# Normed columns kept in memory for two gate stages and the stick projections, with transposed stick queries and keys

## The reference

```python
hx = rms_norm(x, norm_g[i]) * (1.0 + scale_x) + shift_x      # layer 0: window attention, layer 1: latent attention
# both layers: o = attention(projections of hx);  y = (o * silu(hx @ W_gate)) @ W_out
x = x + gate_x * y

# second block, even mixer
hn = rmsnorm(h, norm_gain[0])
qa, ka, va, ga, qb, kb, vb, gb = split(hn @ w_in, 8)         # eight parts of 512 columns
o_a = retention(rotary(qa), rotary(ka), va)
o_b = stick_breaking(qb, kb, vb)                             # four heads of 128
mixed = concat([o_a * silu(ga), o_b * silu(gb)]) @ w_out
```

## Time and profile before

| | us |
|---|---|
| median of 3 runs | 4573.9 (4572.03 to 4575.41) |
| the profiled execution | 4582.14, of which its span is 4580.4 |
| window gate stage, first to last instruction | 635.4 to 973.8 |
| latent gate stage | 1887.9 to 2160.9 |
| stick projections | 2474.9 to 2732.9 |

### The profile page before, as it was taken

The page is one execution under the profiler, slowest core; times in us unless marked ns, Lnnn a source line. Parts: engine busy times, 40 slices in busy tenths (PEclk is TensorE's granted clock), DMA queues, the critical chain, the costliest instruction groups (busy, mean ns, idle before and its releaser), DMA issues. The chain is left out here.

```text
span 4580.4 us, 70575 instructions
## 1 busy us (share of the span) xinstructions
PE 4184.7 (91%) x29426; PEld 2468.8 (54%) x29426; DVE 1581.9 (35%) x2947; ACT 1361.1 (30%) x2322; POOL 318.1 (7%) x143
## 2 busy tenths in 40 slices
PE   7999989989989999898998988998999978888798
PEld 1447854445556666543554446443444467788443
DVE  0336642123135444322332017012222256666111
ACT  0117752212245555321222228111222121211132
POOL 0000000000000000000000000000000027565000
PEclk9999999999999999999999999998999989999899
DMA  7100020041241111001102001104111121211300
GB/s 268 61 1 4 2 84 0 0 85 47 86 125 32 32 32 32 5 0 35 57 0 74 0 1 48 45 0 175 46 46 55 51 102 41 67 50 40 138 14 23
DMA packets 158778, 229.26 MB, mean 50 GB/s; under 512 B 79750, under 2 KB 90182, under 8 KB 158536
## 3 DMA queue, kind: packets, MB, share of 16 engines
q1 hardware_dynamic: 158542, 225.78, 14.9%
HBM read 175.21 MB, written 50.54 MB: 49 GB/s over the span
## 5 line engine op out<-in xcount | busy, mean ns | idle before, releaser
L221 PE MATMUL psum<-rp_w,rp_mixed 128*128 128x512 f32 x1024 | 448.2, 596 | 6.6 <-issue 3.6
L221 PEld LDWEIGHTS psum<-rp_w,rp_mixed 128*128 128x128 f32 x1024 | 194.3, 191 | 248.3 <-issue 242.0
L1353 PE MATMUL psum<-la_kT,la_qT 96*128 96x512 f32 (+1 forms) x768 | 300.6, 528 | 15.4 <-DMA la_v<-latent_v 12.5
L2296 POOL TENSOR_TENSOR rs_kk<-rs_k,rs_k_k 128x1024 f32<-128x1024 f32 x7 | 16.5, 2362 | 3833.4 <-DVE rs_k L2640 3707.7
L1295 DVE TENSOR_SCALAR_CACHE_REDUCE la_s<-psum 128x1280 f32<-128x1280 f32 x128 | 190.9, 1492 | 238.1 <-PE psum L1353 238.1
L221 PE MATMUL psum<-output_wo,pg_oT 128*128 128x512 f32 x512 | 230.8, 610 | 12.2 <-DMA output_wo<-in_even_w_out_dram 6.0
L221 PE MATMUL psum<-output_wg,pg_xT 128*128 128x512 f32 x512 | 227.4, 602 | 7.3 <-ACT pg_xT L1927 7.3
L221 PE MATMUL psum<-retention_w,sp_hT 128*128 128x512 f32 x512 | 223.3, 597 | 10.2 <-ACT even_o L1656 8.7
L221 PE MATMUL psum<-retention_w,ret_hT 128*128 128x512 f32 x512 | 222.9, 596 | 3.3 <-DMA retention_w<-in_even_w_in_dram 1.7
L1283 ACT ACTIVATE la_pT<-psum 128x512 f32<-128x512 f32 x256 | 138.9, 595 | 289.0 <-PE psum L1371 289.0
L1353 PEld LDWEIGHTS psum<-la_kT,la_qT 96*128 96x128 f32 x768 | 137.1, 192 | 141.9 <-issue 129.0
(11 more groups left out here) (410 smaller groups left out, 7106.3 us busy)
## 6 DMA issues: line engine op xcount, KB each, us to landing
ada_slots<-in_ada_w_dram SPq DMA_DIRECT2D x12, 2048.0 KB, 19.5
rwkv_raw<-x_rows SPq DMA_DIRECT2D x48, 512.0 KB, 2.6
retention_w<-in_even_w_in_dram SPq DMA_DIRECT2D x8, 2048.0 KB, 13.2
rp_w<-in_odd_w_in_dram SPq DMA_DIRECT2D x4, 4096.0 KB, 29.0
output_wg<-in_ple_gate_dram SPq DMA_DIRECT2D x2, 4096.0 KB, 23.5
latent_v<-lp_v SPq DMA_DIRECT2D x10, 512.0 KB, 2.6
la_kT<-latent_kT SPq DMA_DIRECT2D x16, 320.0 KB, 4.6
la_v<-latent_v SPq DMA_DIRECT2D x16, 320.0 KB, 5.3
```

Of the source, the lines that this page charges most:

```text
L221: last = pe.matmul(out[:, c:c + w], left[:, k, :], right[:, k, c:c + w], start=(k == 0), stop=(k == kd - 1))
L1353: last = pe.matmul(s_banks[:, c:c + n], qT[:, s, q * P:(q + 1) * P], kT[:, s, c:c + n], start=True, stop=True)
L2296: eng.tensor_tensor(kk[:, :], k[s][:, :], k_k[:, :], ALU.mult).then_inc(q["kk_made"], 1)
```

## The change

It stores columns and uses them again, and drops the norm from three stages.

- `window_qkv`: the two-slot hT becomes a buffer of the layer. SP stores the columns of tiles 0 to 7 to memory; tiles 8 and 9 stay in the two slots. DVE waits for the store before it writes a slot again.
- `window_attend`: SP loads the gate's first weight half, wg0, behind its own two loads.
- `gate_and_project`: no norm. The tiles go 8, 9, 0 to 7 in the window layer. SP loads the columns of tile i into slot i % 2 once gate product i - 2 is done. The gate has two PSUM pairs, ogT two slots. PE's order becomes transposes of og(i), gate product i+2, output product i; the last tile's transposes come ahead of the output product before it, into the gate pair that is free.
- `latent_projections`: SP stores the columns of the eight x tiles, DVE waits for the store as above. `latent_attention` prefetches the first two tiles' columns behind the gate weights.
- `retention`: SP stores the columns of tiles 0 to 6; tile 7 stays in SBUF. DVE waits for the store of tile i before it makes the columns of i+1.
- `stick_projections`: no norm and no transposes. hT holds four tiles (128 x 8 x 512). v and gate are made per tile as before; q and k are made transposed, with the weight of one head stationary and 512 rows of columns streaming, straight into qT and kT.

```diff
+class Columns:
+    def load(self, sp, i):
+        sp.dma_start(self.at[:, i % 2, :, :], self.sources[i]).then_inc(self.arrived[i % 2], 16)
+    def wait(self, pe, i):
+        loads = sum(self.sources[k] is not None for k in range(i % 2, i + 1, 2))
+        if loads:
+            pe.wait_ge(self.arrived[i % 2], loads * 16)
...
 # window_qkv, SP, behind its weight loads (latent_projections: the same store ahead of each step's others)
+                for i in range(NT - 2):
+                    sp.wait_ge(hT_steps, (i + 1) * 2)
+                    sp.dma_start(hT_dram[i], hT[:, i % 2, :, :]).then_inc(hT_stored[i % 2], 16)
 # window_qkv and latent_projections, DVE, columns(i)
                     if i >= 2:
                         dve.wait_ge(kv_made, i - 1)
+                        dve.wait_ge(hT_stored[i % 2], (i // 2) * 16)
...
 # gate_and_project
-        front = Front(nc, mem, name, core, None, 0, core.banks(0, 2))
-        g_banks, ogT_banks, y_banks = core.banks(2, 2), core.banks(4, 2), core.banks(6, 2)
+        g_sets, y_banks = [core.banks(0, 2), core.banks(2, 2)], core.banks(6, 2)
+        ogT_banks = lambda i: core.banks(4, 2) if i + 1 < count else g_sets[count % 2]
...
+                weights.load(sp, late)
+                for i in range(2, count):
+                    sp.wait_ge(g_made, i - 1)
+                    columns.load(sp, i)
...
 # ACT
+                silus(0)
+                for i in range(count):
+                    if i + 1 < count:
+                        silus(i + 1)
                     move(i)
 # DVE
                 gates(0)
                 dve.wait_ge(gate_in, 16 * len(conds))
+                for i in range(count):
+                    if i + 1 < count:
+                        gates(i + 1)
                     residual(i)
 # PE
                 def output_product(i):
                     pe.wait_ge(ogT_read, i + 1)
-                    pe.wait_ge(y_steps, i * Y_STEPS)
+                    if i:
+                        pe.wait_ge(y_steps, (i - 1) * Y_STEPS + 1)
...
                 gate_product(0)
+                gate_product(1)
                 pe.wait_ge(weights.arrived["wo"], 16)
+                for i in range(count):
+                    if i < count - 1:
+                        transpose_og(i)
+                    if i + 2 < count:
+                        gate_product(i + 2)
+                    if i == count - 2:
+                        transpose_og(count - 1)
                     output_product(i)
...
 # retention, DVE, ahead of dve_columns(i + 1)
+                    dve.wait_ge(hT_stored, i * 16 + 16)
...
 # stick_projections, PE
+                def rows(n):
...
+                    product(pe, v_banks[n % 2], left, w_v[:, :, :], zv_made)
+                    product(pe, g_banks[n % 2], left, w_g[:, :, :], zg_made)
+                def turned(n):
+                    c, h, which = turns[n]
+                    if n >= 4:
+                        pe.wait_ge(turned_moved, n - 3)
+                    w = (w_q, w_k)[which]
+                    for k in range(KD):
+                        last = pe.matmul(turned_banks[n % 4], w[:, k, h * R_DIM:(h + 1) * R_DIM], hT[:, k, :], start=(k == 0), stop=(k == KD - 1))
+                    last.then_inc(turned_made, 1)
...
+                rows(0)
...
+                for n in range(len(turns) // 2):
+                    turned(n)
+                for n in range(1, X_TILES):
+                    rows(n)
+                for t in range(CHUNK):
+                    pe.wait_ge(hT_in[t], 32)
+                for n in range(len(turns) // 2, len(turns)):
+                    turned(n)
```

More of the change, by code:

```diff
@@ L373, in window_qkv @@
              "rope_k", "q_turned", "k_turned", "qT_moved", "kT_moved"))
+        hT_stored = [nc.alloc_semaphore(f"{name}_hT_stored{k}") for k in range(2)]
         cond = lambda i: 1 if i < CTX_TILES else 0
@@ L726, in _, with gate_and_project @@
                         values(u - 2)
-def gate_and_project(nc, core, name, o, tiles, layer, weights, load, gate_rows):
+def gate_and_project(nc, core, name, o, tiles, weights, late, columns, gate_rows):
     with ExitStack() as mem:
@@ L1408, in _, with retention @@
                 passes(pe, run)
-def retention(nc, core, a, weights, next_weights, o):
+def retention(nc, core, a, weights, next_weights, o, hT, hT_dram):
     name = "ret"
@@ L1451, in _ @@
                 weights.load(sp, ("w1", "w2", "w3"))
+                for i in range(X_TILES - 1):
+                    sp.wait_ge(front.hT_made, i + 1)
+                    sp.dma_start(hT_dram[i], hT[:, :, :]).then_inc(hT_stored, 16)
+                sp.wait_ge(hT_stored, (X_TILES - 1) * 16)
                 sp.wait_ge(qk_made, X_TILES)
@@ L1643, in _, with load @@
             def _(sp):
-                sp.dma_start(norm_columns[:, :], columns_of(a["norm_gain_2"][0]), allow_slow_non_contiguous=True).then_inc(norm_in, 16)
+                def load(t):
+                    sp.dma_start(hT[:, :, columns(t)], hT_dram[t]).then_inc(hT_in[t % CHUNK], 16)
+                for t in range(CHUNK):
+                    load(t)
+                sp.wait_ge(turned_made, len(turns) // 2)
+                for t in range(CHUNK, LAST):
+                    sp.wait_ge(zg_made, order.index(t - CHUNK) + 1)
+                    load(t)
@@ L1658, in _ @@
-                with act.Fori(0, X_TILES - 1) as i:
-                    front.act_stat(act, i + 1, x(i + 1))
-                    move(i)
-                move(X_TILES - 1)
+                for n, t in enumerate(order):
+                    act.wait_ge(zv_made, n + 1)
+                    act.activation(v[:, t, :], v_banks[n % 2], ACT.Copy).then_inc(v_moved, 1)
+                    act.wait_ge(zg_made, n + 1)
+                    act.activation(o[:, t, W:], g_banks[n % 2], ACT.Silu).then_inc(g_moved, 1)
@@ L1678, in _ @@
-                move(X_TILES - 1)
+                for n, (c, h, which) in enumerate(turns):
+                    if n == len(turns) // 2:
+                        dve.wait_ge(zg_made, order.index(CHUNK - 1) + 1)
+                        dve.tensor_copy(hT[:, :, columns(LAST)], last_hT[:, :, :]).then_inc(hT_in[LAST % CHUNK], 16)
+                    dve.wait_ge(turned_made, n + 1)
+                    dst = (qT, kT)[which]
+                    dve.tensor_copy(dst[:, h, c * CHUNK * P:(c + 1) * CHUNK * P], turned_banks[n % 4]).then_inc(turned_moved, 1)
@@ L2878, in program @@
             o = layer.enter_context(nc.sbuf_tensor("window_o", [P, ALL_TILES, D], F32))
+            hT = layer.enter_context(nc.sbuf_tensor("window_hT", [P, 2, KD, P], F32))
+            window_hT = nc.dram_tensor("window_hT_rows", [ALL_TILES - 2, P, KD, P], F32, kind="Internal").ap()
+            gate_tiles = [ALL_TILES - 2, ALL_TILES - 1] + list(range(ALL_TILES - 2))
+            columns = Columns(nc, "window_columns", hT, [None, None] + [window_hT[t] for t in range(ALL_TILES - 2)])
+            first = Weights(nc, layer, "window_first", {"wg0": halves("wg", a["a_w_in"][0][:, D + 2 * A_KV * A_DIM:])["wg0"]})
             with ExitStack() as keys:
```

198 lines of the change are left out of this document (83 added, 115 removed).

## The result

| | before | after |
|---|---|---|
| median, us | 4574.2 (4 runs, 4572.03 to 4575.41) | 4449.24 (4 runs, 4444.99 to 4460.8) |
| profiled execution, us | 4582.14 | 4446.34 |
| span, us | 4580.4 | 4444.3 |
| mean granted clock | 0.960 | 0.969 |

The ratio is 0.9736, with a 95% interval of 0.9721 to 0.9752: faster, by 125 us against 115 forecast.

The account below looks back on a forecast made before the run. PE, busy 91% of the span, was taken to bound the kernel: gains of 45.5 (window gate), 36.4 (latent gate) and 35.2 (stick) less 2.0 for the clock make 115.1, so 4573.9 - 115.1 = 4458.8 us; range 4450 to 4475.

Parts of the forecast that it names:

- The products and cycles: Gate stages: PE runs at 13.73 us a product and 0.88 a set of og transposes, cycles of 28.3.
- The slow starts: Start of the three stages: first products at low clock, 2.0 us window gate, 2.6 latent gate, 2.0 stick.
- The new end waits: End of each gate stage: PE waits 3.1 us for DVE's og product and 1.5 for y's PSUM pair.
- The clock after new gaps: Gate stages: slow products behind the 3.1 wait, charged 1.0 us a stage, 2.0 together; bounds 0 and 8.
- The other reading of the clock: Both gate stages' end waits: each sufficient idle gap restarts PE at half rate, charging 8 us, sum 4465.
- The turned products: Stick projections: transposed q and k products cost the same as before, 0.43 us pitch; stage gain 35.2.
- The transfers at nothing: 23 stores and 21 loads of columns lie beside PE's work, costed at 0 us; upper bound 171.
- The claim with the least slack: Window gate start: wg1 lands about 8.1 us after issue, covered by a slow half product of 9.
- this sign of being right: In the three changed stages: no DMA among the releasers of PE.
- og waits in every cycle: Gate stages: og's transposes wait 3.1 us for DVE each cycle, 50 more, 4509; chance 0.06.
- The late loads: Stick stage's first loads or wg1 come late, 5 to 15 us, 4464 to 4474; chance 0.08.
- "I keep" the 8.2: Whole kernel: the profiled execution's 8.2 us above the median is kept, so 4573.9 less 115.1 gives 4458.8.

Follow-up runs that it names:

- Experiment 4: The kernel after, with both end waits of each gate stage removed by a second og slot, reordering and a free PSUM pair; 4441.53 us, ratio 0.9706.
- experiments 1: The kernel after, with retention and stick projections of the kernel before, so only the gate stages changed; 4491.52 us, ratio 0.9812.
- 5: The kernel after, with gate-stage column loads from the fourth on issued only when output product i - 3 is done; 4496.71 us, ratio 0.9841.
- 6: The kernel after, with each of the 23 column stores issued a second time into other memory and all waits for both; 4457.64 us, ratio 0.9743.
- Experiment 8: The kernel after, with q and k in stick projections made by rows, moved by ACT and transposed by PE as before; 4477.92 us, ratio 0.9797.

## Why the prediction was right, and where its edge was not

Stage by stage, on the profiled executions, with the clock's charge in each gate stage:

| stage | before | forecast | after | gain forecast | gain measured |
|---|---|---|---|---|---|
| window gate | 338.4 | 293.9 | 294.3 | 44.5 | 44.1 |
| latent gate | 273.0 | 237.6 | 235.9 | 35.4 | 37.1 |
| stick projections | 258.0 | 222.7 | 223.2 | 35.2 | 34.8 |
| sum | | | | 115.1 | 116.0 |

These are the first profiles of each kernel. Over all three of each, in the order of the last table, before takes 338.4, 340.2, 337.8 (window), 273.0, 273.1, 273.1 (latent) and 258.0, 258.2, 258.3 (stick); after takes 294.3, 294.5, 294.5, then 235.9, 237.2, 238.9, then 223.2, 223.6, 223.2. The gains of the means are 44.4, 35.7 and 34.8, together 114.9 against 115.1 forecast.

- **The products and cycles**: 13.73 a product and 0.88 a set of og transposes gave 28.34, and 28.34 was measured.
- **The slow starts**: 2.0, 2.6 and 2.0 in the sum, 6.6. The window stage's first half product took 1.8 more than one at full clock; the stick stage's first 32 instructions 16.44, 2.5 more than 13.90. The latent stage's first 64 took 29.40, 1.7 more than 27.73. Together 6.0.
- **The new end waits**: 3.1 and 1.5 forecast, 2.84 and 1.41 measured in both gate stages, released by the DVE steps that were named. Experiment 4 took them away, and the two stages together became 9.7 shorter than in the first profile of after and 11.3 shorter than in the mean of three.
- **The clock after new gaps**: 1.0 a stage taken, 2.0 together. In the first profile of after it was 1.8 in the window stage (0.83 in the transposes, 0.94 in the product behind them) and nothing in the latent stage behind the same 2.84. In the second and third profile both stages were slow behind it, by 1.6 and 1.4, then by 1.7 and 3.1. So after paid 1.8, 3.0 and 4.8 in three executions, and that the first comes so near the 2.0 is luck. Seven profiles have these two waits in both stages (after's three, experiments 1, 5, 6 and 8): 11 of their 14 waits of 2.84 were followed by slow work, which makes 1.4 on average over the 14, and none of their 14 waits of 1.41. The 0.8 a gap that the charge started from was itself low: it counts the slow products of seven cycles (5.7) but not the norm's transposes ahead of them, which took 1.27, 1.69 and 1.50 at three of these gaps and 1.09 at the others.
- **The other reading of the clock** was 8 for the four waits, as the prediction applied the Trainium skill, TensorE: Matmul & The Clock Gate, section "HAM oscillation — how this bites in real kernels", where a matmul burst starts cold after each long wait. That was too wide a use of the section: the waits that it speaks of are longer than any of these four, so by its own words none of them would have been charged. The traces of this case decide: slow work behind most waits of 2.84, none behind those of 1.41, 1.8 to 4.8 us in all. The charge of 2 was nearer to that than 8, and it was low.
- **The turned products**: 0.43 each, as the latent projections' row said, and the columns were in time. Experiment 8 shows that the transposed form is worth 22 of the stage's 34.8, which the sum, made for the stage as a whole, had not parted.
- **The transfers at nothing**: DVE waited for no store, and the three stages that store are no longer for it: counted to the start of the next stage, `window_qkv` takes 237.2 to 238.7 before and 237.2 after, `latent_projections` 292.2 to 292.4 and 291.2 to 291.3, `retention` 312.3 to 312.9 and 311.8 to 313.1. Making 12 loads late cost 43.5, so they were hidden and not free. From the third on, a load in the window stage was issued 43 us before its product (819.4 for the product at 862.17), not the 28 of the prediction; the first had 14.4 (649.4 for 663.78), and that was enough. The claim with the least slack was wg1: it landed 8.5 after its issue, and PE passed on to it 8.64 after its own start, since its first half product ran slow. At full clock that is 6.87, and PE would have waited some 1.6 for wg1. In the second and third profile wg1 landed after 8.9 and 8.8, and PE went on to it 0.27 and 0.14 later: there this sign of being right, no DMA among what PE waits for, failed by that much.
- **The rival "og waits in every cycle"** fell: one such wait a stage. **The late loads** did not come.

The three profiles of each kernel reach the scan at 3686.8 and 3569.7 in the mean: 117.1 apart, 2 from the forecast. Of these 2, some 1.1 is `latent_projections`, which the prediction left unchanged and which is shorter in every profile of after (why was not looked into). Another 1.1 is no gain of the change: `stick_breaking`, which was not touched, took 408.1 in the second profile of before and 404.4 to 404.8 in the other five. Two small errors are in the sum itself: the terms of the window stage add up to 292.7, not to the 292.9 that it gives, and 4458.8 less 6.6 is 4452, not 4451.

**The step that failed is the range.** It was added up from the terms of the change, 4451 to 4471 and a little beyond, as if the rest of the program stood still. "I keep" the 8.2 by which the profiled execution lay above the median was the sentence that hid it. In the profiles such differences are mostly the scan stage's own variation, and 591.1 was among its longer ones; for executions without a profile this is not shown. Single executions of after spread over 4442.93 to 4470.68 (10 runs, median 4451.0, mean 4454.8), and medians of four or five move with them: 4449.24 and 4449.94. Mean against mean, 4573.1 (the 15 runs of before of the last series) less 4454.8 makes 118.3, close to the 117.1 of the positions; the 1.2 between them is what is left for a change of the scan itself, less than the 3 or so by which a mean of these 10 runs is uncertain. The other 6 or 7 us by which the medians of the result differ more are that variation, and not a gain of the change. The lower end should have stood some 8 us lower for it, the same distance that the two numbers given at the start already had between them.

## What to carry to other kernels

When PE is the bound and waits once a cycle, look first at what stands ahead of the releasing step on its engine's queue: one moved line gave half of what the rebuilt gate stages gained, and the rebuilt order then left two more waits of the same kind at its ends, worth 10 to 12 us. Storing an intermediate of 512 KB and loading it again cost nothing here while each load had at least a product's time of cover (14 us), and 3.6 us a load when it had only the transposes' 0.9: the rest of its latency, and at five of twelve gaps a slow start. Judge a change by the positions of stages in the trace where an untouched stage varies by more than the change's uncertainty, and put that variation into the range.

## What was not expected of the hardware

- A stage of 13728 small matmuls took 569.6 to 594.2 us in 13 profiles of unchanged code, with the granted clock between 0.91 and 0.95, while after's three profiles lay within 0.7 of each other over all that comes ahead of the latent gate stage (1841.2 to 1841.9).
- The same 2.84 gap of PE, in the same place of the same kernel, was followed by a full-speed product in one execution (13.90) and by slow ones in two others (14.38 and 16.03); with gaps of 2.64 and 2.63 one cycle apart, the half product behind took 8.83 and 7.13.
- A 512 KB load that had nothing ahead of it landed in 3.4 to 3.5 and a store in 2.6; those that were queued behind weights took up to 21.7 and 17.0, and none of these was waited for.
